# Two layers of a transformer on one core: the first gather ahead of the bias products, and two slabs of the first expert pair in buffers outside the ring

## The reference

```python
lat_mix = jnp.concatenate([gqa_attention(...), diff_attention(...)], axis=-1)
x = x + gt1 * (lat_mix @ w_o[l])
x = x + gt2 * moe_ffn(modulate(rms_norm(x, g_ffn[l]), sh2, sc2), w_router[l], b_router[l],
                      w_in[l], b_in[l], w_out[l], b_out[l])

def moe_ffn(h, ...):                      # 32 experts, 4 for each token
    logits = xt @ w_router + b_router
    top_val, top_idx = lax.top_k(logits, TOP_K)
    gates = jax.nn.softmax(top_val, axis=-1)
    ...                                   # per expert: clamped SwiGLU of x w_in[e] + b_in[e],
                                          # times w_out[e], plus b_out[e], weighted by its gate
```

## Time and profile before

| | us |
|---|---|
| median of 3 runs (2252.59 to 2258.3) | 2254.33 |
| the profiled execution | 2251.53 |
| its span | 2249.7 |
| TensorE busy (matmul) | 2091.3 (93%) |
| VectorE / ScalarE busy | 549.1 / 401.1 |
| granted TensorE clock, mean | 0.972 |

### The profile page before, as it was taken

How to read it: one execution, slowest core, us unless ns; L and a number is a source line. 1 busy time by engine, 2 the same in 40 slices (tenths; PEclk the granted TensorE clock), 3 DMA queues, 4 the chain that set the end, 5 groups by cost and what they waited for, 6 DMA issues and landing times.

```text
span 2249.7 us, 25319 instructions
## 1 busy us (share of the span) xinstructions
PE 2091.3 (93%) x10390; PEld 1346.5 (60%) x10390; DVE 549.1 (24%) x1168; ACT 401.1 (18%) x743; POOL 174.2 (8%) x225
## 2 busy tenths in 40 slices
PE   6999879999989899899899989999999999989998
PEld 4644654444444444334444467677888888878887
DVE  1065332221222221112222252113102404510321
ACT  3124211111101111111111120111103224320211
POOL 0000000000000000000000000000191961000000
PEclk8999979999999999999999999999999999999999
DMA  9549829999999999999999974468043333534320
GB/s 362 187 151 387 325 100 417 417 410 418 417 416 418 418 418 418 418 418 418 418 418 417 415 263 158 153 219 343 18 150 136 129 145 119 203 116 156 125 110 19
DMA packets 164372, 627.79 MB, mean 279 GB/s; under 512 B 5232, under 2 KB 9456, under 8 KB 127824
## 3 DMA queue, kind: packets, MB, share of 16 engines
q1 hardware_dynamic: 163840, 625.39, 70.7%
q0 software_dynamic: 464, 1.44, 0.2%
HBM read 625.76 MB, written 1.05 MB: 279 GB/s over the span
## 4 chain that ended last, share of the span: by engine, by line
PE 74%; DMA 14%; DVE 7%; issue 2%; ACT 2%; SPq 1%; DVEq 0%; ACTq 0%
PE psum L918 30%; PE psum L1215 21%; DMA ring<-in_w_in_dram 13%; PE psum L929 2%; PE psum L953 2%; PE psum L1191 2%; PE psum L1235 2%; DVE arena L2154 1%; PE psum L1447 1%; PE psum L1299 1%; PE psum L1473 1%; PE psum L1103 1%; DMA ring<-in_w_ada_dram 1%; DVE arena L2169 1%; SPq L800 1%
## 5 line engine op out<-in xcount | busy, mean ns | idle before, releaser
L1215 PE MATMUL psum<-ring,arena 128*64 128x512 f32 x3168 | 712.1, 607 | 77.0 <-DMA ring<-in_w_in_dram 76.1
L918 PE MATMUL psum<-arena,ring 128*128 128x256 f32 (+1 forms) x3072 | 687.3, 387 | 14.7 <-ACT arena L1548 14.7
L918 PEld LDWEIGHTS psum<-arena,ring 128*128 128x128 f32 x3072 | 588.4, 192 | 110.9 <-issue 29.8
L1215 PEld LDWEIGHTS psum<-ring,arena 128*64 128x64 f32 x3168 | 240.1, 140 | 535.4 <-issue 479.7
L1664 ACT ACTIVATE arena<-psum 128x512 f32<-128x512 f32 (+1 forms) x155 | 88.5, 571 | 832.2 <-PE psum L1215 709.8
L2154 DVE TENSOR_TENSOR arena<-psum,arena 128x512 f32<-128x512 f32 (+1 forms) x68 | 44.3, 671 | 427.6 <-PE psum L1235 427.6
L1584 ACT ACTIVATE arena<-psum 128x512 f32<-128x512 f32 (+1 forms) x68 | 38.7, 572 | 374.2 <-PE psum L918 182.1
L2141 DVE TENSOR_SCALAR arena<-consts,arena 128x64 f32<-128x64 f32 (+1 forms) x68 | 16.7, 310 | 337.9 <-PE psum L1215 337.9
L2408 DVE SCALAR_TENSOR_TENSOR consts<-psum,smalls,consts 128x255 f32<-128x255 f32 (+1 forms) x88 | 38.4, 478 | 246.4 <-ACT consts L1796 245.7
L2555 POOL DMA_DIRECT2D arena<-in_pos_dram x1 | 0.6, 577 | 1034.6 <-DVE tiny L2233 1034.6
L1191 PE MATMUL psum<-arena 128*128 128x256 f32 x288 | 70.3, 387 | 4.3 <-DVE arena L2130 3.3
(11 more groups left out here) (341 smaller groups left out, 1562.8 us busy)
## 6 DMA issues: line engine op xcount, KB each, us to landing
ring<-in_w_in_dram SPq DMA_DIRECT2D x132, 2048.0 KB, 15.1
ring<-in_w_out_dram SPq DMA_DIRECT2D x66, 2048.0 KB, 18.0
ring<-in_w_ada_dram SPq DMA_DIRECT2D x36, 2048.0 KB, 13.8
ring<-in_w_up_dram SPq DMA_DIRECT2D x22, 2048.0 KB, 7.8
ring<-in_w_ret_dram SPq DMA_DIRECT2D x12, 2048.0 KB, 12.6
ring<-in_w_down_dram SPq DMA_DIRECT2D x16, 1408.0 KB, 5.8
ring<-in_w_qkv_dram SPq DMA_DIRECT2D x4, 2048.0 KB, 18.5
ring<-in_w_rout_dram SPq DMA_DIRECT2D x4, 2048.0 KB, 14.2
```

Of the source, the lines that this page charges most:

```text
L918: ins = nc.tensor.matmul(bank(c)[:, at:at + n], w[:, k, m * P:m * P + P], r, start=(k == 0), stop=(k == k_tiles - 1))
L1215: ins = nc.tensor.matmul(psum[at:at + CAP, p, :], act[:, k, CAP * e:CAP * e + CAP], w[:, kk, n0:n0 + BANK], start=(k < 3 - halves), stop=( ...
```

## The change

- SP: the first pair's slab 2 is loaded into the arena at h_cat, glu and lin (`early_w[0]`), once ("ob", 3) is done; its slab 3 in two loads of 1 MB into h_moe and sq, once ("htok", 3) is done. The ring holds ten slabs of this pair instead of twelve (`slot_at`, `MOE_0`), and their waits are for other counts of rows_done. Pair 0 is written out ahead of the loop on each engine that needs it.
- TensorE: all four tiles m of wo0 and wo1 are taken over mix tiles 0 to 3 ahead of mix_ready (the halves of a bank share one start and one stop flag), where it was two. The bias products come behind the first gather, into banks 4 to 7. h_cat and gsel are turned by transposes instead of matmuls with the identity, except in an overflow job.
- ScalarE: the exp of the gates stands ahead of the copies of htok.
- VectorE: select ahead of the memsets, the copies of the bias products behind them, the list of overflow jobs behind pair 0.
- GpSimd: the router's weights are loaded at q_ready 1, in attention, to the end of the arena.

```diff
-MOE_SLABS = 12 * PAIRS
+EARLY_SLABS = 2
+MOE_SLABS = 12 * PAIRS - EARLY_SLABS
+MOE_0 = SLABS_1 - EARLY_SLABS
+def slot_at(n):
+    return (n + 2) % RING
...
+        at = KD * T + TT * D + KD * T + KD * P
+        early_w = [arena[:, at:at + SLAB].rearrange("p (a b) -> p a b", a=UP_TILES), (flat(h_moe), flat(sq))]
...
-        w_rt = cut(KD, E)
+        w_rt = arena[:, ARENA - KD * E:].rearrange("p (a b) -> p a b", b=E)
...
-            for j in range(12):
-                if j < RING:
-                    slab_left(sp, SLAB_KEYS[SLABS_1 + j - RING])
+            for q in range(12 - EARLY_SLABS):
+                j = q if q < 2 else q + EARLY_SLABS
+                if q == 4:
+                    read_ready(sp, ("ob", 3))
+                    sp.dma_start(early_w[0], expert_source(0, 1)).then_inc(early_in[0], 16)
+                if q == RING:
+                    read_ready(sp, ("htok", 3))
+                    for kk, out in enumerate(early_w[1]):
+                        sp.dma_start(out, expert_source(1, 1)[:, kk, :]).then_inc(early_in[1], 16)
+                if q < RING:
+                    slab_left(sp, SLAB_KEYS[SLABS_1 + q - RING])
                 else:
-                    sp.wait_ge(moe.rows_done, (j - RING) // 2 + 1)
-                load(SLABS_1 + j, expert_source(j % 2, j // 2))
+                    sp.wait_ge(moe.rows_done, 1 if q < 8 else 3)
+                load(SLABS_1 + q, expert_source(j % 2, j // 2))
...
-                    load(SLABS_1 + j, expert_source(i * 2 + j % 2, j // 2))
+                    load(MOE_0 + j, expert_source(i * 2 + j % 2, j // 2))
...
                     ins = nc.tensor.matmul(half(key, m % 2), wo[n][:, k, m * P:m * P + P], mix[:, k, :],
-                                           start=(k == 0), stop=(k == KD - 1))
+                                           start=(k == 0 and m % 2 == 0), stop=(k == KD - 1 and m % 2 == 1))
                 if k1 == KD and m % 2:
                     end(ins)
             arrived("wo0")
             for i in range(4):
                 copied(pe, ("oa", i))
-            for m in (0, 2):
+            for m in range(4):
                 wo_tile(0, m, 0, 4)
             for i in range(2):
                 pe.wait_ge(qk_square, 3 + i)
                 nc.tensor.matmul(psum[:, 4 + i, :], con("ones"), flat(sq[:, 2 * i:2 * i + 2, :]),
                                  start=True, stop=True).then_inc(onorm_ready, 1)
             arrived("wo1")
-            for m in (0, 2):
+            for m in range(4):
                 wo_tile(1, m, 0, 4)
             pe.wait_ge(mix_ready, 1)
             for n in range(2):
-                for m in (0, 2):
+                for m in range(4):
                     wo_tile(n, m, 4, KD)
-                    wo_tile(n, m + 1, 0, KD)
...
-                begin(("bout", c))
-                if c == 0:
-                    pe.wait_ge(bout_in, 16)
-                    copied(pe, ("gates", 0))
-                for m in range(2):
-                    k = 2 * c + m
-                    ins = nc.tensor.matmul(half(("bout", c), m), b_out_sb[0:E, k * P:k * P + P],
-                                           gates_t[0:E, :], start=True, stop=True)
-                end(ins)
-            for c in range(4):
-                copied(pe, ("bout", c))
+                copied(pe, ("htok", c))
+            copied(pe, ("pos", 0))
...
-                        ins = nc.tensor.matmul(psum[:, 6 + c % 2, m * P:m * P + width],
-                                               h_cat[:, c, m * P:m * P + P],
-                                               con("ident" if halves == 2 else "fold"), start=True, stop=True)
+                        out, of = psum[:, 6 + c % 2, m * P:m * P + width], h_cat[:, c, m * P:m * P + P]
+                        if halves == 2:
+                            ins = nc.tensor.transpose(out, of, con("ident"))
+                        else:
+                            ins = nc.tensor.matmul(out, of, con("fold"), start=True, stop=True)
...
-                    ins = nc.tensor.matmul(psum[:, 2, t * P:t * P + P], gsel[:, t, :],
-                                           con("ident"), start=True, stop=True)
+                    ins = nc.tensor.transpose(psum[:, 2, t * P:t * P + P], gsel[:, t, :], con("ident"))
...
             gather(moe, 2, 1)
-            with pe.Fori(0, PAIRS) as i:
+            pe.wait_ge(bout_in, 16)
+            copied(pe, ("gates", 0))
+            for k in range(KD):
+                ins = nc.tensor.matmul(psum[:, 4 + k // 2, T * (k % 2):T * (k % 2) + T],
+                                       b_out_sb[0:E, k * P:k * P + P], gates_t[0:E, :], start=True, stop=True)
+                if k % 2:
+                    ins.then_inc(bout_ready, 1)
+            def tile_in_ring(j, k_tiles, kk):
+                return in_rows(slot_at(MOE_0 + j), k_tiles)[:, kk, :]
+            def first_full(j):
+                if j in (2, 3):
+                    pe.wait_ge(early_in[j - 2], 16 * (j - 1))
+                else:
+                    n = SLABS_1 + j if j < 2 else MOE_0 + j
+                    pe.wait_ge(ring_full[slot_at(n)], 16 * (n // RING + 1))
+            def first_tile(j, k_tiles, kk):
+                if j == 2:
+                    return early_w[0][:, kk, :]
+                if j == 3:
+                    return early_w[1][kk]
+                return in_rows(slot_at(SLABS_1 + j if j < 2 else MOE_0 + j), k_tiles)[:, kk, :]
+            experts(moe, 2, 0, first_full, first_tile)
+            with pe.Fori(1, PAIRS) as i:
                 def full(j):
-                    n = SLABS_1 + j
-                    pe.wait_ge(ring_full[n % RING], i * 32 + 16 * (n // RING + 1))
-                experts(moe, 2, i, full, lambda j: (SLABS_1 + j) % RING)
+                    n = MOE_0 + j
+                    pe.wait_ge(ring_full[slot_at(n)], i * 32 + 16 * (n // RING + 1))
+                experts(moe, 2, i, full, tile_in_ring)
...
             apply(2)
+            act.wait_ge(top_ready, 1)
+            nc.scalar.activation(top_e[:, :, 0:TOP_K], top_e[:, :, 0:TOP_K], ACT.Exp).then_inc(top_exp, 1)
             for c in range(4):
                 copy(("htok", c), h_tok[:, c // 2, BANK * (c % 2):BANK * (c % 2) + BANK])
-            act.wait_ge(top_ready, 1)
-            nc.scalar.activation(top_e[:, :, 0:TOP_K], top_e[:, :, 0:TOP_K], ACT.Exp).then_inc(top_exp, 1)
...
-            for c in range(4):
-                key = ("bout", c)
-                read_ready(dve, key)
-                read_done(V.tensor_copy(y_moe[:, 2 * c:2 * c + 2, :], two(bank(key))), key)
-            for c in range(4):
-                copied(dve, ("bout", c))
...
+            select(moe, 2, (0, 1), 0)
             own.link(V.memset(y_slot, 0.0))
             own.link(V.memset(g_slot, 0.0))
             for c in range(2):
+                dve.sem_inc(moe.y_copied, 1)
+            for c in range(4):
+                dve.wait_ge(bout_ready, c + 1)
+                V.tensor_copy(y_moe[:, 2 * c:2 * c + 2, :], two(psum[:, 4 + c, :])).then_inc(bout_read, 1)
+            dve.wait_ge(bout_read, 4)
+            for c in range(2):
                 dve.sem_inc(moe.x_free[c], 1)
-            for c in range(2):
-                dve.sem_inc(moe.y_copied, 1)
-            select(moe, 2, (0, 1), 0)
+            experts(moe, 2, 0, (0, 1), 0, (2, 3), 0)
...
-            with dve.Fori(0, PAIRS - 1) as i:
+            with dve.Fori(1, PAIRS - 1) as i:
...
+            pool.wait_ge(q_ready, 1)
+            pool.dma_start(w_rt, w_router.rearrange("(k p) n -> p k n", p=P)).then_inc(router_in, 16)
             pool.wait_ge(x_ready, 1)
-            pool.dma_start(w_rt, w_router.rearrange("(k p) n -> p k n", p=P)).then_inc(router_in, 16)
```

29 lines of the change are left out of this document (17 added, 12 removed).

## The result

| us | before | after |
|---|---|---|
| median of 4 runs each (lowest to highest) | 2256.14 (2252.59 to 2258.3) | 2233.11 (2232.05 to 2234.11) |
| the profiled execution, its span | 2251.53, 2249.7 | 2233.53, 2231.7 |
| TensorE busy (matmul) | 2091.3 | 2053.5 |
| granted TensorE clock, mean | 0.972 | 0.978 |

The ratio is 0.9899 [0.9882, 0.9917]. Forecast were 2237.9 us for the median, of 2230.5 to 2245, and 2235.1 for the profiled execution. Between the medians lie 23.0 us, between the profiled executions 18.0.

A forecast was written before the change was run, and what follows sets the result against it. The expert pairs were taken as bound by DMA transfers, 5.02 us a slab. Terms -14.2, -1.4 and -0.85 sum to -16.45: 2235.1 us profiled, plus 2.8 for the median, 2237.9; range 2230.5 to 2245.

The forecast's parts named there:

- Step 1: Output projection, more passes ahead of mix_ready: ends 4.7 us earlier if the clock is kept, 3.6 if it falls again.
- Step 2: Router's weights asked for at q_ready instead of x_ready: router ends at 294.7 against 295.52, -0.8 us.
- Steps 3 and 4: Exp ahead of htok copies, about -0.1 us; select directly behind slot numbers, so gather starts 7.3 us after router, not 18.87.
- Step 5: Bias products moved between gather and up(0): 3.56 us at full clock, in place of 0.86 us of ScalarE copy.
- The rival of 7.17 us: Clock rises late, bias products run at half: +3.6 us, +1.6 for gather, 2243.1 us in all; chance 0.15.
- The sum of steps 1 to 5: Start of the first up(0), called u: 306.6 instead of 320.83 us, -14.2 us.
- Step 6: Two slabs of the first pair loaded early: -1.4 us, not 10, because stream gaps of 3.9 and 4.8 us open.
- Step 7: Transposes replacing identity matmuls for h_cat and gsel: nothing in stream-bound pairs, -0.85 us behind the last pair's last slab.
- The first rival: Clock does not fall before the router, so router's second half, htok and gather run faster: -3.8 us, 2234.1; chance 0.15.
- The two slabs in full: Early slabs in the expert stream give their full 10 us, without gaps: 2229.3 us; chance 0.06.
- The gain that doesn't arrive: First up(0) moves but the expert stream does not start with it: 2248 to 2258 us; chance 0.04.
- the slower case: Expert pairs lose the clock at transposes and stop being stream-bound: 6.2 us come through, 14 times, 2325 us; chance 0.02.

The follow-up runs named there:

- warm: Changed kernel plus short stretches of dummy matmuls ahead of TensorE's waits, in both blocks: 2224.96 us, ratio 0.9872 to the kernel before.
- after_again: The changed kernel itself, unedited, run again as a control: 2233.23 us, ratio 0.9913 to the kernel before.
- no_early: Changed kernel with both early slabs of the first pair back in the ring, with the old waits: 2238.29 us, ratio 0.9936 to the kernel before.
- three_early: Changed kernel plus a third early slab, the second pair's slab 2, loaded into h_moe and sq: 2230.21 us, ratio 0.9902 to the kernel before.
- turn_by_matmul: Changed kernel with h_cat and gsel turned by matmuls with the identity again: 2238.5 us, ratio 0.9933 to the kernel before.
- warm_turn_by_matmul: warm with h_cat and gsel turned by matmuls with the identity again: 2228.76 us, ratio 0.9888 to the kernel before.
- bias_first: Changed kernel with the bias products ahead of the first gather again: 2235.63 us, ratio 0.9922 to the kernel before.
- warm_no_early: warm with all twelve slabs of the first pair in the ring: 2229.57 us, ratio 0.9888 to the kernel before.
- wo_as_before: Changed kernel with the old projection order, 16 and 16 passes ahead of mix_ready and 96 behind: 2236.16 us, ratio 0.9929 to the kernel before.
- warm_three: warm plus the third early slab: 2221.65 us, ratio 0.9855 to the kernel before.

## Why the prediction was right

The time came 4.8 us under the forecast, within the range and of the right sign, by the mechanism named: the start of up(0) moved, the stream moved with it, and the two slabs gave little. One reading ahead of the steps is wrong, without a price: the DMA engines aren't idle from 241 to 320 us. The rows of the prediction's own group 6 have them at a share of 1.02 and 1.00 up to 263 us and at 0.84 over 283 to 288.5; they are idle only from there on. Step by step, between the profiled executions:

- *Step 1, the projection, -4.7:* measured -2.05 (277.42 against 279.46 for its end). **This term was mis-sized**: "I take it as kept" was wrong. The clock fell in the 3.5 us wait too, 0.80 over 256 to 262 and 0.86 over the next 16, and 64 passes took 17.10 in place of 14.24. The prediction's other bound for the step, 3.6, assumed the same loss as before (22.51 for 96 passes in place of 21.4, 1.1 us); here the loss is 2.9. The wait itself was about as long as the 3.2 us worked out. In warm, where the clock is held, they took 14.08.
- *Step 2, the router's weights, -0.8:* -0.77 (292.70 for its end against 295.52, beside the -2.05). No run undoes this step or step 3 by itself; both are read from positions alone.
- *Steps 3 and 4, from the router's end to the gather, 7.3 in place of 18.87:* 6.56 (299.26 - 292.70). The gather took 3.81, not 5.58: "half clock first" was wrong, since the clock was back to 1.00 before it. So 0.7 and 1.8 more than forecast.
- *Step 5, the bias products at full, +2.8 net:* 3.65 us of them, +2.78. The rival of 7.17 us fell: the clock had risen. But at that spot, see below, another clock loss waits that I hadn't seen.
- *The sum of steps 1 to 5:* 306.71 against 306.6. The 2.65 too much in step 1 and the 2.5 too little in step 4 cancel. The hit on u is therefore partly luck, and honest only to some 2.5 us.
- *Step 6, the two slabs, -1.4 and not 10:* -1.44, with both gaps in the stretches at the places worked out (u + 18 and u + 42 forecast, u + 19 and u + 43 found), their lengths 3.7 and 4.8 where 3.9 and 4.8 were worked out, and 2.0 of gain behind both at up(3) of the second pair (79.0 us behind u in place of 81.1), less by the last pair. After_again has only 0.5 at the last pair (896.38), so a single pair of profiles gives the -1.44 to about 1 us. no_early gives 1.6. three_early fills the first gap and gets 5.2. The two edits lean on each other, as the 0.85 that the prediction takes into its second gap has it: with matmuls by the identity this gap is 5.4 and 5.8 us, with transposes 4.4 to 4.8. In the stream early slabs without the transposes measure 897.2, no better than before (896.85), and transposes without early slabs 897.0. That fits, but these are two profiles each, with a grain of 1.0 us.
- *Step 7, the transposes, -0.85 in the last pair:* -1.02, and no price in the pairs. The rule cited from the Trainium skill, TensorE: Matmul & The Clock Gate, PE-mode transpose, would have the pairs lose the clock behind the transposes. The granted clock over a pair's 59 us is 0.97 after and 0.97 before, and a pair lasts (1229.74 - 385.73)/14 = 60.29 us. Over 820 us of the pairs, before (first line) and after, it is 0.98 in both:

```profile
400.83:1220.83 820.00, 749.09 (x3782) 346.53 (x3784) 160.01 (x312) 105.00 (x154) 0.00 (x0) 0.98 1.02 417
...
386.71:1206.71 820.00, 724.29 (x3540) 315.28 (x3538) 158.79 (x312) 105.07 (x154) 0.00 (x0) 0.98 1.02 417
```

  The clock does fall now and then in the pairs: behind the first up block, a block that ran partly at half, most often an up(3), is found in 2 places in before, 2 in turn_by_matmul and 5 in warm_turn_by_matmul, all three with matmuls by the identity, and in 1 to 4 in the eleven profiles with transposes. So these losses come with either way of turning, and no run here shows the loss in each pair.
- *The first rival*, a clock that doesn't fall before the router, didn't hold: it was 0.50 from 286 to 293. Its price for the gather came anyway, by a rise afterwards. *The two slabs in full*: no, though three_early shows how to come nearer. *The gain that doesn't arrive* and *the slower case*: nothing of either.

The remaining 4.8 us: by the profiled executions the kernel is 1.6 under the 2235.1 forecast, which is the -2.7 of clock in the second block (1.65 of it in the stage of 112 passes; where the other 1.0 lies wasn't found) less the 1.32 that up(3) of the last pair lost. The other 3.2 are the offset of 2.8 that I added for the median: it belonged to the runs of before, whose mean clock varies more (0.970 to 0.976, against 0.977 to 0.980), and the changed kernel's median lies 0.4 under its profiled run.

## What to carry to other kernels

Before giving a stream bound by its rate a head start, list when each slot of the ring comes free again: an early transfer counts only as far as no later wait opens a gap behind it, and the last of these waits says what the edit is worth. On a path with idle stretches of some 3 us, the granted clock is a term of its own for every step behind them; price each step at both levels, and compare edits by positions in the profiles, since runs of one program spread by more than a step is worth. An offset between a profiled run and a median isn't a property to be carried over to the changed kernel.

## What the runs showed of the hardware

- **The clock falls in stretches that differ from run to run.** In attention TensorE has 0.28 us of work from 149 to 152 us, in the profile of after as in that of no_early; the clock there is 1.00 in one and 0.86 in the other. In five profiles the clock over 153 to 241 us is 0.99 or 1.00 and w_o starts at 239.7 to 241.3, in three (no_early, bias_first, turn_by_matmul) it is 0.96 or 0.97 and w_o starts at 243.6 to 245.2. With five dummy matmuls there it started at 239.2 to 241.1 in all six warm profiles. Keeping the engine busy ahead of waits was worth 8.3 us in the median.
- **Behind 3.65 us of matmuls over 32 rows at full clock, the clock fell in five of ten profiles**, with TensorE never idle: 0.50 for about 3 us of the first up block, which took 29.3 to 29.5 us in place of 27.62 (no_early, turn_by_matmul, three_early, warm, warm_no_early), while in as many it didn't (after, after_again, wo_as_before, warm_three, warm_turn_by_matmul). In the two profiles with the products taken in two halves between halves of the gather, it was 1.00. Two profiles don't prove the cure, and what sets the five that fell apart from the five that didn't isn't known.
- **Full transposes are one pass, matmuls with the identity two**: four blocks in 0.60 to 0.66 us, 0.15 to 0.17 each, against eight in 2.00 us, 0.25 each, at no visible price in clock.
- **A half clock in a pair bound by DMA can cost DMA time.** Behind three up(3) of 8.78 to 10.10 us the DMA engines fell to 199 to 224 GB/s for 3 to 4.5 us, 27 to 29 us after its start (after_again once, turn_by_matmul twice), 1.5 to 2.1 us lost each time. In all three SP issued its next two loads, for which it had waited, only within the stretch (594.91, 419.20 and 902.56 us); that the half clock made it late is argued from the order of events.
